# The recurrence of a hybrid GLA and SSD layer: segments as difference and minimum with zero, the mask multiplied into the product of B and C once a tile

## The reference

```python
a_cum = jnp.cumsum(dt * A.reshape(G, Hg), axis=2)
causal = jnp.tril(jnp.ones((L, L), dtype=bool))
seg = a_cum[:, :, :, None] - a_cum[:, :, None]
decay_ij = jnp.exp(jnp.where(causal[:, :, None, None], seg, -jnp.inf))
cb = jnp.einsum('bcign,bcjgn->bcijg', Cm, Bm)
w = cb[..., None] * decay_ij * dt[:, :, None]
y = jnp.einsum('bcijgh,bcjghp->bcighp', w, x)
```

## Time and profile before

| | |
|---|---|
| median of 3 runs | 1679.96 us (1679.74 to 1680.04) |
| profiled execution | 1679.87 us, its span 1678.1 us |
| PE busy | 1610.5 us, 96% |
| DVE busy | 1049.9 us, 63% |
| ACT busy | 840.7 us, 50% |
| POOL busy | 398.5 us, 24% |
| segments, L1792 | 256 instructions, 68.6 us |
| `decay` times `cb`, L1757 | 32 instructions, 38.9 us |
| mean granted clock of PE | 0.991 of full speed |

### The profile page before, as it was taken

How to read it: one execution, slowest core, us unless ns; L and a number is a source line. 1 busy time by engine, 2 the same in 40 slices (tenths; PEclk the granted TensorE clock), 3 DMA queues, 4 the chain that set the end, 5 groups by cost and what they waited for, 6 DMA issues and landing times. The chain is left out here.

```text
span 1678.1 us, 27425 instructions
## 1 busy us (share of the span) xinstructions
PE 1610.5 (96%) x9990; PEld 1387.0 (83%) x9990; DVE 1049.9 (63%) x1754; ACT 840.7 (50%) x1496; POOL 398.5 (24%) x449
## 2 busy tenths in 40 slices
PE   4999999999999999998999998999999999999997
PEld 4888888888888888887888887888888878888886
DVE  4545454455444554456777777867777755785886
ACT  5655555545544554464444555555454554234332
POOL 2311000101322222200232222223222220450523
PEclk9999999999999999999999999999999999999999
DMA  9423442264433533334122125323212326765886
GB/s 331 126 95 108 137 124 70 74 193 145 157 126 130 190 121 129 124 104 145 70 77 76 69 81 149 115 73 111 76 69 75 102 99 212 238 237 170 304 275 198
DMA packets 131358, 231.14 MB, mean 138 GB/s; under 512 B 9907, under 2 KB 81859, under 8 KB 126134
## 3 DMA queue, kind: packets, MB, share of 16 engines
q1 hardware_dynamic: 121830, 189.71, 34.9%
q10 hardware_dynamic: 8592, 39.85, 6.4%
q0 software_dynamic: 832, 0.22, 0.3%
HBM read 177.05 MB, written 52.70 MB: 137 GB/s over the span
## 5 line engine op out<-in xcount | busy, mean ns | idle before, releaser
L1150 PE MATMUL ps<-hl,w 128*128 128x512 f32 x1488 | 372.8, 399 | 0.1
L1150 PEld LDWEIGHTS ps<-hl,w 128*128 128x128 f32 x1488 | 273.9, 188 | 56.2 <-issue 1.4
L1858 PE MATMUL ps<-hl,w 128*128 128x256 f32 x2304 | 295.5, 288 | 6.8 <-ACT c_acc L1599 6.8
L1858 PEld LDWEIGHTS ps<-hl,w 128*128 128x128 f32 x2304 | 282.8, 193 | 14.9 <-issue 14.9
L1156 PE MATMUL ps<-w,hl 128*128 128x256 f32 x1536 | 200.6, 287 | 0.0
L1156 PEld LDWEIGHTS ps<-w,hl 128*128 128x128 f32 x1536 | 190.6, 191 | 2.3
L1731 DVE SCALAR_TENSOR_TENSOR c_acc<-c_before,conv_col,c_acc 128x256 f32<-128x256 f32 x288 | 161.6, 562 | 38.5 <-ACT c_acc L1599 31.5
L1862 PE MATMUL ps<-hl 128*128 128x512 f32 x768 | 178.5, 391 | 0.0
L1862 PEld LDWEIGHTS ps<-hl 128*128 128x128 f32 x768 | 143.0, 188 | 29.2
L2247 PE MATMUL ps<-w,hl 128*128 128x512 f32 x720 | 164.1, 389 | 0.0
L2247 PEld LDWEIGHTS ps<-w,hl 128*128 128x128 f32 x720 | 135.0, 188 | 28.2 <-issue 0.2
(11 more groups left out here) (247 smaller groups left out, 2611.3 us busy)
## 6 DMA issues: line engine op xcount, KB each, us to landing
x_sb<-h SPq DMA_DIRECT2D x52, 512.0 KB, 3.9
w_raw<-in_w_in SPq DMA_DIRECT2D x42, 512.0 KB, 5.0
c_ac<-step_sums ACTq DMA_DIRECT2D x16, 1024.0 KB, 4.7
d_a_raw<-mixed_in SPq DMA_DIRECT2D x29, 512.0 KB, 4.1
c_h_raw<-h SPq DMA_DIRECT2D x56, 256.0 KB, 2.9
d_a_raw<-mixed_in SPq DMA_DIRECT2D x11, 1024.0 KB, 5.0
w_sums<-late ACTq DMA_DIRECT2D x8, 1280.0 KB
w_raw<-w_sums SPq DMA_DIRECT2D x40, 256.0 KB, 3.6
```

Source lines behind the costliest of these rows:

```text
L1150: mm = pe.matmul(ps[:, PROJ + u % 2, :], w[:, u, k, a, :], hl[:, par, k, b, :], start=(k == 0 and i == 0), stop=(k == KT - 1 and i == 2))
L1858: mm = pe.matmul(ps[:, PROJ + u % 2, 0:B2], w[:, u, k, a, :], hl[:, par, k, b, :], start=(k == 0 and i == 0), stop=(k == KT - 1 and i == 2))
```

## The change

`past` becomes a mask of ones (allowed) and zeros. The segments lose it: they are now the difference and the minimum with zero, one tensor input and one scalar per row. For pairs outside the past exp then gives 1 instead of 0, and the zero comes from a new product: `cb` is copied out of PSUM multiplied by the mask, once a tile, into a new buffer `c_cb` in SBUF. `decay` is multiplied by that buffer instead of by PSUM. The new product signals a new semaphore, for which DVE itself waits before the next instruction.

```diff
+        cb = sb("c_cb", [P, P])
...
-        ac_loaded = sem("c_ac_loaded"); consts_ready = sem("c_consts")
+        cb_ready = sem("c_cb_ready"); ac_loaded = sem("c_ac_loaded"); consts_ready = sem("c_consts")
...
-            pool.memset(past[:, :], 0.0).then_inc(consts_ready, 1)
+            pool.memset(past[:, :], 1.0).then_inc(consts_ready, 1)
...
-            pool.affine_select(out=past[:, :], in_=past[:, :], compare_op=ALU.is_ge, fill=-1e30,
+            pool.affine_select(out=past[:, :], in_=past[:, :], compare_op=ALU.is_ge, fill=0.0,
                                base=0, pattern=[[1, P]], channel_multiplier=-1).then_inc(consts_ready, 1)
...
                 dve.wait_ge(bc_done, m + 1)
                 dve.wait_ge(decay_ready, r + 1)
-                dve.tensor_tensor(decay[:, :, t * P:(t + 1) * P], ps[:, BC, NS:NS + P].unsqueeze(1).broadcast_to([P, HG, P]),
+                dve.tensor_tensor(cb[:, :], ps[:, BC, NS:NS + P], past[:, :], ALU.mult).then_inc(cb_ready, 1)
+                dve.wait_ge(cb_ready, m + 1)
+                dve.tensor_tensor(decay[:, :, t * P:(t + 1) * P], cb[:, :].unsqueeze(1).broadcast_to([P, HG, P]),
                                   decay[:, :, t * P:(t + 1) * P], ALU.mult)
...
-                        last = dve.scalar_tensor_tensor(
-                            out=decay[:, h, t * P:(t + 1) * P], in0=ac[:, h, t * P:(t + 1) * P], scalar=own,
-                            in1=past[:, :], op0=ALU.subtract, op1=ALU.min)
+                        last = dve.tensor_scalar(decay[:, h, t * P:(t + 1) * P], ac[:, h, t * P:(t + 1) * P], own, 0.0,
+                                                 ALU.subtract, ALU.min)
```

## The result

| | before | changed |
|---|---|---|
| median of 8 runs | 1680.0 us (1678.3 to 1683.2) | 1685.8 us (1683.7 to 1688.4) |
| changed by before | | 1.0036 (95% interval 1.0027 to 1.0045) |
| profiled execution | 1679.87 us, span 1678.1 | 1688.38 us, span 1686.6 |

What follows compares the result with a forecast made beforehand. PE, busy 96% of the span, was taken to bound the kernel. Segments 0, exposed steps 2.9 and tail 2.0 summed to 4.9 us on 1679.87: 1684.9 us, 0.29% more, range 1680.6 to 1689.

Steps and rivals of the forecast that it cites:

- Segments, 0 us: Segments in every step: 286 ns instead of 348, the saving lying wholly in DVE's idle time, worth 0 us.
- The mask's product, 0.32 us later: New product of cb and mask, once per tile: 285 ns plus semaphore, making the product with `decay` 0.32 us later.
- the rival's 0.8: Rival: POOL does not hold up the product with `decay`; only 0.32 us counts, 0.8 us in all, 1680.8; chance 0.21.
- The product queues with POOL: Product with `decay`, now two SBUF inputs, takes turns with POOL's `xend` and `decayed`; work behind is 0.98 us late.
- about 1.6 us: Sign to look for: length of the product with `decay` in second tiles, well above 1216 ns.
- Ordinary steps at 0: Twelve steps where PE waits for nothing: 0.98 us lateness against 1.3 us of tolerance, so 0 us.
- Three exposed steps, 0.98 us each: Last step of group 0, step after it, last step of group 1: PE already waits, so 2.9 us together.
- Tail, 2.0 us: After step 15 both tiles lie on the path, each 0.98 us late: together 2.0 us.
- a rival at 0.12: Rival: PE's granted clock falls in the tail behind a 2.8 us wait, costing 1 or 2.6 us; 1686 to 1688.
- POOL goes first twice: Rival: `decayed` takes the port ahead of the product, PE waits for `btok` in every ordinary step; 1694, chance 0.10.
- Faster: Rival: shorter segments release ACT's exp, up to 16 us gained against 4.9 paid; 1669, chance 0.07.

Runs made afterwards that it cites:

- e2: Kernel before with only the new segments, the causal mask left out: median 1680.3 us, ratio to before 1.0006.
- e3: Changed kernel with the segments back in their old form, the mask still multiplied into cb in SBUF: median 1686.0 us, ratio to before 1.0042.
- e1: Changed kernel with the masked cb written back to its place in PSUM instead of a buffer in SBUF: median 1682.1 us, ratio to before 1.0011.
- e5: Changed kernel with POOL computing `decayed` ahead of `xend` in second tiles: median 1683.5 us, ratio to before 1.0028.
- e9: Changed kernel as it is, run once more for a second profile: 1685.4 us in one run.
- e4: Changed kernel with POOL computing the first tile's rstd between the second tile's `decayed` and its skip: median 1680.0 us, ratio to before 1.0004.
- e8: Changed kernel with masked cb in PSUM, first tile's rstd before second tile's skip, and `decayed` ahead of `xend` in second tiles: median 1679.6 us, ratio to before 0.9994.
- e7: Changed kernel with masked cb in PSUM and POOL computing the first tile's rstd before the second tile's skip: median 1676.7 us, ratio to before 0.9983.

## Why the prediction was right, step by step

- *Segments, 0 us.* Right, alone (e2) and in the changed kernel (e3). The size was right too: 282 ns for 286.
- *The mask's product, 0.32 us later.* Right: 281 ns, and the product starts 0.32 us behind it (845.63 to 845.95). By itself it costs 0.6 us (e1), against the rival's 0.8.
- *The product queues with POOL.* Right, and shown by e1, which only moves the buffer: 5.3 of the 6.0 us of the stage go. That turns are taken is in the trace (1.49 and 2.03 us), and e5 shows that the second turn is most of what is paid: 0.6 of 1 us go at an exposed step when POOL has nothing queued behind `xend`, although `btok` is as late as before. The text announced "about 1.6 us" for the product in second tiles; its own working gives 843.45 to 844.93, 1.48 us, and that was measured.
- *Ordinary steps at 0.* Right but for 0.05 us, and with less to spare than it looks: in the step of the earlier trace rows `c_yn` ended 0.08 us before PE took it up (855.74 to 855.82), where 0.05 is the latency and 0.38 us were forecast. That step is 36.62 us long instead of 36.57, in changed, e3 and e9 alike.
- *Three exposed steps, 0.98 us each.* In the profile 1.38, 1.07 and, with the 0.5 us of the tail's first tile taken off, 0.98. The 1.38 was 0.90 in e9; the weights' arrival varies by half a microsecond. The size is right in all three, but in the first, the last step of group 0, the way is another than forecast: PE's turn there does not hang on rstd. It follows ACT's split of a weight block, which stands ahead of `c_yn` on ACT and waits for its DMA. Before, then changed (the turn before is in the earlier trace rows):

```profile
1036.14 2.53 SPq L1432 DMA_DIRECT2D w_raw<-in_w_in  x2
...
1040.62 1.06 ACT L1575 ACTIVATE w<-w_raw 128x1024 fp32r<-128x1024 f32 x1 [0.71 <-DMA w_raw<-in_w_in]
```

```profile
1039.81 2.53 SPq L1433 DMA_DIRECT2D w_raw<-in_w_in  x2
...
1044.57 1.06 ACT L1576 ACTIVATE w<-w_raw 128x1024 fp32r<-128x1024 f32 x1 [1.37 <-DMA w_raw<-in_w_in]
...
1046.81 0.66 PE L1920 MATMUL ps<-ident,c_yn 128*128 128x128 f32 x4 [1.62 <-ACT c_yn L1631]
```

  In all eleven profiles the turn starts 2.2 us after this split has begun, and the step is longer by what the split is later, within 0.04 us. DVE's splits behind the queue free the buffers 1.1 us later, so SyncE asks for the weights 1.14 us later (18.39 instead of 17.25 us into the step), and they took 4.76 us instead of 4.48: together the 1.4. In e4 rstd was early and the step stayed as it was. The queue still sets the step, through a transfer that the prediction did not look at; that the size came out near 0.98 us is in part luck.
- *Tail, 2.0 us.* This is the term that was mis-sized: 0.5 and 2.0, together 2.5 us. The half microsecond more goes with the clock, which I had as a rival at 0.12: it fell in the tail in all four profiles in which the SBUF product stands with rstd at its old place (changed, e3, e5, e9). What it cost can be read from POOL's add of the skip, from which a chain over rstd, `c_yn` and `c_y` leads to the last turn. Before, then changed:

```profile
1366.93 1.28 POOL L1535 TENSOR_TENSOR c_yi<-c_yi,c_xd 128x512 f32<-128x512 f32 x1 [1.29 <-DVE c_yi L1771]
```

```profile
1374.85 1.26 POOL L1536 TENSOR_TENSOR c_yi<-c_yi,c_xd 128x512 f32<-128x512 f32 x1 [1.29 <-DVE c_yi L1774]
```

  From its end to the last turn it is 5.85 us before, where PE waited 0.52 us for `c_y`, and 6.40 in the changed kernel, where PE waited for nothing and `c_y` came no later after the add (4.6 us in both). So the difference, 0.55 us, goes to the clock, and without it the tail's term is close to the 2.0 forecast. The price was less than the 1 us said, since PE would have waited there for `c_y`. In e5 the same stretch took 7.16 us, 1.3 more than before, which is why its tail gave nothing.
- *POOL goes first twice* did not occur in 32 tiles, nor in any other run. *Faster*: excluded by e2 and e3.

So the 6.0 us of the stage are the 4.9 forecast, 0.5 more in the tail, and about 0.5 by which the weights came later in this profile than in e9. The interval of the measured ratio (0.27% to 0.45%) holds the 0.29% of the forecast.

What stays open is the clock. PE's wait of 2.8 us in the tail was the same in e4, and the clock stayed up:

```profile
1366.30:1374.00 7.70, 7.25 (x35) 1.00 0.00 0
```

In e8 it fell behind one of 1.9 us, and in e7, with a wait of 1.9 us at the same place, it did not. No experiment here holds everything else still, so the fall is a risk that comes with waits of this size, not a result of one length.

## What to carry to other kernels

Count, for each VectorE instruction that an edit touches, how many of its tensor inputs lie in SBUF. Here the step from one to two made an instruction take turns with GpSimd: it waited for the instruction that ran there, and GpSimd's next one then waited for it, so the work behind both was late by more than the edit's own length. That was 1 us at each exposed place for a 0.3 us instruction, and a buffer in PSUM instead of SBUF took nine tenths of the stage's cost away. And look for the few places where the bounding engine already waits: in this kernel the edit was free everywhere else, and there it was paid in full. At such a place look at every chain that ends in the wait, the refill of a buffer by DMA too: in the last step of group 0 it was that one.

## What the runs showed of the hardware

- The mask's product, a VectorE instruction with one input in PSUM, one in SBUF and its output in PSUM runs at about the speed of one that writes SBUF: 289 and 281 ns for 128 columns (e1, changed). It did not queue with GpSimd: 286 to 290 ns in all 32 tiles, in second tiles beside `xend`.
- The product of 1024 columns takes 1224 ns from SBUF and SBUF with GpSimd idle, 1216 from PSUM and SBUF, 1.49 us beside one GpSimd instruction. The turns alternated in the rows shown, and the product took at most 1.50 us in every tile: the waiting one ended about 1.09 us (the product) or 0.90 us (`xend` or `decayed`, 512 columns) after the other.
- The granted clock of PE can fall to the lower level for 3.4 us behind waits of 1.9 us and more, and did so in the tail in five of eleven profiles; behind other waits of the same length it stayed up (1.9 us in e7, 2.2 in changed and e3, 2.8 in e4). Where no other wait covered it, it cost 1.5 us (e8's tail, e9's step after group 0).
